# A third pair of one-hot buffers, and a new home for half of the last tile's output weights

## What is computed

```python
a_p = mixer_output(o_lat, h_ml, og, w_kvb[l], mh_norm_g[l], w_o[l], dt)
hp = layer_norm(DN_ALPHA * hp + a_p, ln1_g[l], ln1_b[l])
...
q = jnp.einsum('nd,de->ne', x, w_pq).reshape(n, PEER_HEADS, 2, PEER_DQ // 2)
s = jnp.einsum('nhpc,hpkc->nhpk', q, sub_keys).astype(jnp.float32)
sv, si = lax.top_k(s, PEER_TOPK)
...
experts = e1 * N_KEYS + e2
g = jax.nn.softmax(cv, axis=-1)
act = jax.nn.gelu(jnp.einsum('nhkd,nd->nhk', expert_u[experts], x).astype(jnp.float32))
return jnp.einsum('nhk,nhkd->nd', (g * act).astype(x.dtype), expert_v[experts])
```

## Time and profile before

| what | us |
|---|---|
| median of 3 runs | 2052.14 |
| lowest and highest of them | 2050.41, 2052.62 |
| the profiled execution, its own time | 2047.48 |
| its span, first to last instruction | 2045.8 |
| TensorE busy | 1926.5 (94%) |
| VectorE busy | 1421.1 (69%) |
| ScalarE busy | 686.3 (34%) |
| mean granted TensorE clock | 0.947 of full |

### The profile page before, as it was taken

How to read it: one execution, slowest core, us unless ns; L and a number is a source line. 1 busy time by engine, 2 the same in 40 slices (tenths; PEclk the granted TensorE clock), 3 DMA queues, 4 the chain that set the end, 5 groups by cost and what they waited for, 6 DMA issues and landing times. The chain is left out here.

```text
span 2045.8 us, 28102 instructions
## 1 busy us (share of the span) xinstructions
PE 1926.5 (94%) x9473; PEld 1551.2 (76%) x9473; DVE 1421.1 (69%) x3020; ACT 686.3 (34%) x1168; POOL 278.3 (14%) x229
## 2 busy tenths in 40 slices
PE   6999999899999967888999999999999999999996
PEld 3455456755666636887899889999999999999996
DVE  4112365353268888888888897877888887878786
ACT  1221254200111113666333434443333333333332
POOL 0000000010011000001211111112222222223210
PEclk9989989679899968989999999999999999999998
DMA  7300010361234142339868677779898989888872
GB/s 267 131 0 1 0 37 1 136 233 60 61 120 134 48 168 97 165 165 362 308 238 309 227 302 272 300 285 360 321 359 318 359 320 355 324 343 338 323 270 81
DMA packets 135162, 434.81 MB, mean 213 GB/s; under 512 B 12385, under 2 KB 70162, under 8 KB 111186
## 3 DMA queue, kind: packets, MB, share of 16 engines
q1 hardware_dynamic: 108978, 256.69, 34.4%
q0 software_dynamic: 26112, 177.22, 22.4%
HBM read 399.21 MB, written 34.27 MB: 212 GB/s over the span
## 5 line engine op out<-in xcount | busy, mean ns | idle before, releaser
L1505 POOL DMA_INDIRECT hi<-euv,lo x160 | 243.4, 1521 | 1032.9 <-DVE hi L2079 755.8
L1086 PE MATMUL ps<-xh,ul 128*128 128x384 f32 x1024 | 347.0, 339 | 0.0
L1086 PE MATMUL ps<-xl,uh 128*128 128x384 f32 x1024 | 345.8, 338 | 0.0
L1086 PE MATMUL ps<-xh,uh 128*128 128x384 f32 x1024 | 343.8, 336 | 0.0
L1150 ACT ACTIVATE hi<-ps 128x512 f32<-128x512 f32 (+12 forms) x312 | 176.4, 622 | 297.7 <-PE ps L755 83.8
L1094 PE MATMUL ps<-vh,hh 128*128 128x512 f32 x768 | 241.6, 396 | 7.2 <-DVE hl L2022 7.2
L1094 PE MATMUL ps<-vh,hl 128*128 128x512 f32 x768 | 239.3, 393 | 0.0
L1094 PE MATMUL ps<-vl,hh 128*128 128x512 f32 x768 | 238.1, 391 | 0.0
L1150 ACT ACTIVATE vh<-lo 128x1024 fp32r<-128x1024 f32 x128 | 135.8, 1061 | 268.0 <-PE ps L1094 256.9
L2079 DVE SCALAR_TENSOR_TENSOR hi<-hi,lo 128x1024 f32<-128x1024 f32 x160 | 198.5, 1282 | 7.6
L1086 PEld LDWEIGHTS ps<-xl,uh 128*128 128x128 f32 x1024 | 192.3, 188 | 5.5
(11 more groups left out here) (327 smaller groups left out, 2477.1 us busy)
## 6 DMA issues: line engine op xcount, KB each, us to landing
lo<-eu SPq DMA_DIRECT2D x128, 512.0 KB, 6.1
lo<-ev SPq DMA_DIRECT2D x128, 512.0 KB, 5.4
gates<-hi SPq DMA_DIRECT2D x6, 4096.0 KB, 11.7
hi<-gates SPq DMA_DIRECT2D x62, 384.0 KB, 6.1
hi<-w_pq SPq DMA_DIRECT2D x8, 2048.0 KB, 10.4
hi<-w_in SPq DMA_DIRECT2D x5, 2048.0 KB, 12.7
hi<-cache SPq DMA_DIRECT2D x64, 144.0 KB, 2.8
hi<-cache POOLq DMA_DIRECT2D x64, 144.0 KB, 2.9
```

The costliest lines, as they stand in the source:

```text
L1086: last = nc.tensor.matmul(ps[:, 6 + p, 0:ND * TD], a[p][:, k * 128:(k + 1) * 128], b[:, k, :], start=(k == 0 and b is xh and a is uh), sto ...
L1505: nc.gpsimd.indirect_dma_start(ring[slot].rearrange("p a d -> p (a d)"), None, euv, bass.IndirectOffsetOnAxis(at, 0)).then_inc(r_in[slot], 16)
```

## The change

Four things change together.

- The second half of the last tile's output weights is loaded into a tile of its own, `wo2`, at PB (where pages of the attention's cache and later `oh1[0]` lie), and SP issues it after `sm_done` at 8. It no longer waits for `l1_done`.
- The loads of the tail's queries move to other homes and waits. Load 5 goes to SLOT_B and waits for `l1_done`, load 6 goes to SLOT_A and waits for `wo_ps` and `tk_pick` at 2, load 7 goes to SLOT_B and waits for the first eight query blocks (`pq_ps` at 24).
- The one-hots have three pairs of buffers. VectorE waits for `gm_ps` at 2q - 4, so that a step waits for the one three before it, and the step's pair is number (q + 1) % 3. Before the first step VectorE waits for both halves of the output product in place of the eight query blocks.
- `low_value(0, 1)`, whose output `vl[0]` lies over the new third `oh1`, waits for `gm_ps` at 94.

```diff
-        wob = [view(at, KD, 512) for at in (46436, PB, SLOT_B, SLOT_A)]
+        wob = [view(at, KD, 512) for at in (46436, SLOT_B, SLOT_A, SLOT_B)]
+        wo2 = view(PB, KD, 512)
...
-        oh1 = [view(OH + n * 8 * NK, 8, NK) for n in range(2)]
-        oh2 = [view(OH + (2 + n) * 8 * NK, 8, NK) for n in range(2)]
+        oh1 = [view(at, 8, NK) for at in (OH, OH + 8 * NK, SC + 3 * 2048 + D)]
+        oh2 = [view(at, 8, NK) for at in (OH + 16 * NK, OH + 24 * NK, TK + 3968)]
...
+            sp.wait_ge(s["sm_done"], SB)
+            sp.dma_start(wo2, w_o[:, :, 512:1024]).then_inc(pq_in[0], 16)
+            load_queries(4, 0)
             sp.wait_ge(s["l1_done"], 1)
-            sp.dma_start(wob[2], w_o[:, :, 512:1024]).then_inc(pq_in[0], 16)
-            sp.wait_ge(s["sm_done"], SB)
-            load_queries(4, 0)
             load_queries(5, 1)
             sp.wait_ge(s["wo_ps"], 2 * ST + 2)
+            sp.wait_ge(s["tk_pick"], 2)
             load_queries(6, 0)
-            sp.wait_ge(s["tk_pick"], 2)
+            sp.wait_ge(s["pq_ps"], 3 * PH)
             load_queries(7, 1)
...
-                    last = nc.tensor.matmul(ps[0:TR, 4 + n, :], xmb[:, k, :], (woa, wob[2])[n][:, k, :], start=(k == 0), stop=(k == KD - 1))
+                    last = nc.tensor.matmul(ps[0:TR, 4 + n, :], xmb[:, k, :], (woa, wo2)[n][:, k, :], start=(k == 0), stop=(k == KD - 1))
...
-                n, at = g // 2 % 2, 4 * (g % 2)
+                n, at = (g // 2 + 1) % 3, 4 * (g % 2)
...
-            dve.wait_ge(s["pq_ps"], 3 * PH)
+            dve.wait_ge(s["wo_ps"], 2 * ST + 2)
...
-                if q >= 2:
-                    dve.wait_ge(s["gm_ps"], 2 * q - 2)
-                v.tensor_tensor(oh1[q % 2], bc(iota, 1, 8), bc(ohT[d % 2][:, 0, t:t + 8], 2, NK), ALU.is_equal)
+                n = (q + 1) % 3
+                if q >= 3:
+                    dve.wait_ge(s["gm_ps"], 2 * q - 4)
+                v.tensor_tensor(oh1[n], bc(iota, 1, 8), bc(ohT[d % 2][:, 0, t:t + 8], 2, NK), ALU.is_equal)
...
                 if q == 47:
+                    dve.wait_ge(s["gm_ps"], 94)
                     low_value(0, 1, None)
```

More of the change, by code:

```diff
@@ L2040, in _ @@
                     step(v.tensor_tensor(hi2, hi2, bc(ohT[d % 2][:, 2, half], 2, NK // LOW), ALU.mult))
-                if q >= 2:
-                    dve.wait_ge(s["gm_ps"], 2 * q - 2)
-                v.tensor_tensor(oh1[q % 2], bc(iota, 1, 8), bc(ohT[d % 2][:, 0, t:t + 8], 2, NK), ALU.is_equal)
+                n = (q + 1) % 3
+                if q >= 3:
+                    dve.wait_ge(s["gm_ps"], 2 * q - 4)
+                v.tensor_tensor(oh1[n], bc(iota, 1, 8), bc(ohT[d % 2][:, 0, t:t + 8], 2, NK), ALU.is_equal)
                 at = slice(t % HALF, t % HALF + 8)
-                v.tensor_tensor(oh2[q % 2].rearrange("p t (a b) -> p t a b", b=LOW), bc(hi2[:, at, :], 3, LOW),
+                v.tensor_tensor(oh2[n].rearrange("p t (a b) -> p t a b", b=LOW), bc(hi2[:, at, :], 3, LOW),
                                 bc(lo2[:, at, :], 2, NK // LOW), ALU.mult).then_inc(s["oh_done"], 1)
```

## The result

The changed kernel took 2023.62 us (median of four runs: 2023.45, 2023.50, 2023.75, 2027.99) against 2051.27 us for the kernel before, run beside it. The ratio is 0.987, with a 95% interval of 0.9853 to 0.9887, so it is 23.2 to 30.2 us faster. The forecast of 2031.7 had the sign and both waits that the change was to remove. It did not have what happened in the expert stage behind them.

A forecast was written before the change was run, and what follows sets the result against it. TensorE's two expert-stage products were taken as the bound, so the gain lay in starting that stage earlier: 8.2 us from the weights plus 12.2 from the third pair, 20.4 off 2052.14, gives 2031.7 us, range 2027.5 to 2037.

The forecast's parts named there:

- Part 1: Output product: loading the weights' second half after sm_done removes VectorE's whole wait for the second product, gaining 8.2 us.
- Rival (a): A transfer is late: wo2 landing at 755.4 loses 2.8 us, giving 2034.5, or the end costs 2.95 us, giving 2034; chance 0.08.
- Part 2: One-hot stretch: a third buffer pair removes most of VectorE's waits for TensorE, gaining 12.2 us, bounds 10 and 14.4.
- The debts: VectorE's 12 one-hot waits set against one extra step of 2.27 us: 1.5 of 14.4 us stay, 12.9 go.
- Rival (b): Only one part works: 2043.9 us if the third pair fails, 2039.9 if the weights' part fails; chance 0.05.
- The end loss: End of the one-hots: ScalarE running later behind VectorE costs 0.7 us, bounds 0 and 2.95.
- beyond 3 us: Sign that the forecast is wrong: ScalarE's wait for the expert values, 2.95 us before, grows past 3 us.
- The stage has no gap that the change could close, so its end follows its start.: Expert stage: despite TensorE's 7.2 us of idle time it keeps its length and only begins earlier.
- Rival (d): More gain: part of the expert stage's 7.2 us idle goes too, or fewer slow steps occur: 2027 us; chance 0.04.
- so I take the gain off the median: Starting point: 20.4 us taken off the shown median of 2052.14, not the profiled execution's 2047.48, giving 2031.7.
- Rival (c): Slower: the granted clock stays low through the one-hot stretch, 40 more slow steps costing 53 us, 2085 us; chance 0.03.
- the change makes no such gap longer: Argument against a slower kernel: the clock fell where the gap was 2.93 us, and no such gap grows.

The follow-up runs named there:

- filled kernel: Kernel before, with extra identity products of unused result where TensorE paused ahead of each half tile of one-hots: 2045.76 us, ratio 0.9989.
- weights alone: Changed kernel with two pairs of one-hot buffers as before, keeping the output weights' new home and the moved loads: 2037.58 us, ratio 0.9949 to before.

## Why the prediction was right in its steps and wrong in its number

**Part 1 was right.** Forecast: the wait for the weights goes whole, 8.2 us, and the digits begin at 790.4. Measured: the rows with the waits are gone, and the digits begin 8.3 us sooner behind `sm_done`, in every profile with the new loads. They stood at 791.38 because `sm_done` itself came 1.1 us later in that execution. That VectorE's ranking would lose nothing to the loads beside it held: from the last `sm_done` row to the end of the ranking it is 752.89 - 738.94 = 13.95 us, against 751.76 - 737.80 = 13.96. Load 6 was hidden: its first block, at 809.44, has no idle time ahead of it. Rival (a) did not come in this part.

**Part 2 was right in what it removes.** The debts gave 1.5 us of VectorE's waiting left over, and 0.8 were left, a gain of 13.6 for 12.9. Rival (b) falls with the two parts run apart. The wait of `low_value` for `gm_ps` cost nothing: VectorE's 4.6 us ahead of it are for ScalarE's `vh`. TensorE's wait for VectorE is 22.8 us and not some 30, which costs nothing either.

**The end loss was mis-sized.** The step "I take 0.7, near the 0.56 that shows now" failed. Its bounds of 0 and 2.95 us rested on the values landing at a fixed distance from the rest. They landed 14.0 us behind their issue in place of 10.7, beside gathers that were issued faster, and the loss was 4.40 - 0.56 = 3.8 us in the first profile and about 3 in the others. The step looked for the loss in a later issue, with ScalarE running behind VectorE. The issue came 13.8 us sooner behind the digits and cost nothing. The prediction's own condition, ScalarE's wait "beyond 3 us", was met: 6.33. The one-hots gave 9.8 us in the first profile and 11.0 to 11.4 in the others, for 12.2.

**The stage was the mechanism that was missed.** The step that failed is "The stage has no gap that the change could close, so its end follows its start." The 7.2 us of the earlier trace rows were on the page. 4.92 of them stand in one row, 30 us into the stage, 10 us after the third block's values have come, and issuing that load sooner took 2.1 of the 4.9 us. A stage that begins later against its loads meets them sooner, and the changed kernel begins it after a wait of 4 us. The idle time fell to 1.98 us, and the stage came out 5.2 to 5.3 us shorter in two profiles and 2.6 in one; 1.6 of the 5.3 are the clock at the second idle, which also fell or did not fall in one and the same kernel. Rival (d) named a gain in the stage, with a chance of 0.04 and some 5 us. The filled kernel before has neither the new buffers nor the new homes, and its stage is shorter by as much. The eleven profiles in which no load of values was moved fall into two groups: five with a wait of 3 us and more and an idle of 2.0 us, and six with a wait under 1 us and an idle of 4.7 to 5.8. That the wait ahead is the cause is inferred from this; no experiment changed it alone.

**The starting point was mis-sized.** The gain was taken off 2052.14, the median of three runs. In all, 68 executions of the kernel before are on record, with a median of 2048.73 and a range of 2042.62 to 2052.85. So 2052.14 was near its upper end, and the profiled execution's 2047.48, which the prediction had and did not take as its base, was nearer the middle. The step that failed here is "so I take the gain off the median". Taken off that, the same sum gives 2027.1.

The miss of 2031.7 - 2023.62 = 8.1 us is thus made up of 2052.14 - 2048.73 = 3.4 from the starting point, 3.8 from the gain (24.2 between the medians of all runs, 2048.73 and 2024.52, for 20.4), and 2024.52 - 2023.62 = 0.9 from those four runs. By stretches the gain's 3.8 are the stage's 3.7 and the clock's 1.6 less about 1 in the one-hots, and the rest is the difference between executions.

**The clock did not stay down.** Rival (c) asked for a granted clock at its lower level through the stretch. It stood at 1.00 in most of it, and ScalarE's wait for TensorE fell from 41.5 to 29.0 us. The prediction's count of the stretches below 1.00, twenty of 76, is 22 in that view. The rule of the Trainium skill, "TensorE: Matmul & The Clock Gate", section "A second HAM failure mode: psum-queue depth-cycling", by which small idles between groups that cycle through the banks make the clock swing, is not borne out by this stretch: with idles of 0.22 us its groups went on at 1.00, with two pairs (842 to 844) as with three (820 to 822). Every 0.50 in it stood behind a pause of 2.2 us or more, and not every such pause brought it. The prediction's "the change makes no such gap longer" did not hold at the end: the 4.40 us ahead of the stage are a longer one, and the stage's first products ran at the lower clock behind it.

What stays open: the four runs of before beside the result had a median 2.5 us above that of all its runs. No profile was taken of an execution above 2049.6 us, so no row shows which stretch is longer in those. What decides whether the clock falls behind one and the same idle time, and what makes the stretch ahead of `sm_done` differ between executions, was not looked into.

## What to carry to other kernels

When a wait goes, follow the transfers and not only the engines to the next stage: a load that was just in time for the old start is late for the new one, and an idle row some tens of us into the next stage, with a load at the end of its chain, is part of the sum. A wait moved from inside that stage to the place ahead of it can cost less than it seems, and one removed there may come back inside, so measure both stretches together. Before a difference between two profiles is put down to the change, see whether the clock fell at the same idle times in both. And take a gain off the profiled execution, or off many runs, never off three runs whose median the profile doesn't match.

## What the runs showed of the hardware

**Loads beside gathers.** The load of the first values, issued with a second one of the same 512 KB, was there 7.9 us behind its issue with no gather beside it, and 10.7 us beside gathers of which the first two took 1.94 and 1.96 us to issue. It took 14.0 us beside gathers of 1.42, 0.98 and 1.16 us, and 18.1 us in the filled kernel, where the three behind the first took 0.94 to 1.08 us. Its size was the same each time.

**The same idle time, with and without a fall of the clock.** A pause of 2.88 us ahead of the fifth half tile was followed by 0.50 in one execution of the kernel before and by 1.00 in another. One of 2.93 us brought 0.50 at 828 us in the kernel before and left 1.00 at 821 us in the weights alone. An idle of 1.98 us some 257 to 260 us into the expert stage was followed by 4 us at 0.57 in one profile and at 1.00 in another, for both kernels, and the time from there to the end of the span was 834.43 us with the fall and 832.85 without it, 1.6 us apart, in the first and third profile of the kernel before.

**One kernel, ten us of spread.** The 68 executions of the kernel before lie between 2042.62 and 2052.85 us, and the span goes with the mean granted clock. In the executions listed, 0.951 to 0.952 goes with spans of 2041.1 to 2043.0 us, 0.947 with 2044.8 to 2046.6 and 0.945 with 2047.6 to 2050.4. In its five profiles the last `sm_done` row starts between 737.80 and 739.86 us, the one-hots last 149.9 to 152.5 and the stage 1093.2 to 1095.6. Three runs do not fix a median within a few us here.
